# Index scores of a sparse-attention layer: rectified in place in four PSUM banks, in groups of four with one projection tile behind each

## The reference, cut to what matters

```python
h = x @ w_in                                  # q, k, v, z, qi, ki, wi are column ranges of h
rel = relu(einsum('bthd,bsd->bths', qi_b, ki))             # 8 index heads
score = einsum('bths,bth->bts', rel, wi_b) * INDEX_SCALE   # weighted sum over the heads
score = where(causal, score, -inf)
_, idx = top_k(score, 128)
logits = einsum('bthd,btjd->bthj', q_b, k_sel) * ATTN_SCALE
o = softmax(logits) @ v_sel                   # 16 heads of width 128
out = (o * silu(z)) @ w_out
```

## Time and profile before

| | us |
|---|---|
| Time before, median of 3 runs | 1727.27 (1726.52 to 1730.99) |
| The profiled execution, its own time | 1730.23 |
| Its span in the trace | 1728.2 |
| TensorE busy, share of the span | 1597.8 (92%) |
| VectorE busy | 709.0 (41%) |
| ScalarE busy | 526.3 (30%) |
| GpSimd busy | 589.1 (34%) |

### The profile page before, as it was taken

One profiled execution on the slowest core, in us unless ns is written; L12 is line 12 of the kernel. 1 busy time (PEld: TensorE's weight loads), 2 busy tenths in 40 slices (PEclk: granted clock), 3 DMA queues, 4 the chain that ended last, 5 costly groups with the idle time before them and its releaser, 6 DMA issues. The chain is left out here.

```text
span 1728.2 us, 23481 instructions
## 1 busy us (share of the span) xinstructions
PE 1597.8 (92%) x9937; PEld 1342.5 (78%) x9937; DVE 709.0 (41%) x1399; ACT 526.3 (30%) x850; POOL 589.1 (34%) x244
## 2 busy tenths in 40 slices
PE   6998999999999988999998999899999787968998
PEld 6896885998979854778787997897887643557997
DVE  4031440331163545885544135312401556478524
ACT  3444224332223222244443123433221234331210
POOL 5333320343423274444642423242442350422021
PEclk9998999999999998999999999999999776567999
DMA  4313220224223221220112322442331000020111
GB/s 151 92 55 98 73 72 3 74 94 177 84 74 98 86 85 38 74 93 30 49 49 85 124 74 86 147 105 74 98 98 49 1 1 0 0 69 5 50 50 49
DMA packets 115970, 121.60 MB, mean 70 GB/s; under 512 B 14623, under 2 KB 109833, under 8 KB 115610
## 3 DMA queue, kind: packets, MB, share of 16 engines
q1 hardware_dynamic: 112320, 114.16, 20.9%
q10 hardware_dynamic: 3546, 5.94, 0.9%
HBM read 113.80 MB, written 6.29 MB: 69 GB/s over the span
## 5 line engine op out<-in xcount | busy, mean ns | idle before, releaser
L193 POOL TENSOR_TENSOR w_low<-w_ring,w_high 128x2048 fp32r<-128x2048 f32 (+1 forms) x92 | 419.4, 4559 | 844.7 <-ACT w_high L184 844.7
L209 PE MATMUL ps<-w_high,xT_high 128*128 128x256 f32 (+1 forms) x1056 | 303.6, 287 | 7.8 <-POOL w_low L193 3.4
L209 PE MATMUL ps<-w_high,xT_low 128*128 128x256 f32 (+1 forms) x1056 | 298.4, 283 | 0.0
L209 PE MATMUL ps<-w_low,xT_high 128*128 128x256 f32 (+1 forms) x1056 | 298.3, 282 | 0.0
L184 ACT ACTIVATE w_high<-w_ring 128x2048 fp32r<-128x2048 f32 (+1 forms) x92 | 173.5, 1887 | 369.7 <-PE ps L209 356.6
L209 PE MATMUL ps<-xT_high,w_high 128*128 128x512 f32 (+3 forms) x624 | 253.8, 407 | 8.7 <-DVE mix_a L742 7.7
L209 PE MATMUL ps<-xT_high,w_low 128*128 128x512 f32 (+3 forms) x624 | 249.5, 400 | 0.0
L209 PE MATMUL ps<-xT_low,w_high 128*128 128x512 f32 (+3 forms) x624 | 249.0, 399 | 0.0
L209 PEld LDWEIGHTS ps<-w_high,xT_high 128*128 128x128 f32 x1056 | 202.1, 191 | 15.4 <-POOL w_low L193 8.2
L209 PEld LDWEIGHTS ps<-w_low,xT_high 128*128 128x128 f32 x1056 | 202.0, 191 | 1.8 <-issue 1.7
L209 PEld LDWEIGHTS ps<-w_high,xT_low 128*128 128x128 f32 x1056 | 201.7, 191 | 0.0
(11 more groups left out here) (507 smaller groups left out, 2449.3 us busy)
## 6 DMA issues: line engine op xcount, KB each, us to landing
w_ring<-in_gla_w_in_dram SPq DMA_DIRECT2D x24, 1024.0 KB, 5.3
w_ring<-in_dsa_w_in_dram SPq DMA_DIRECT2D x19, 1024.0 KB, 5.1
w_ring<-in_w_in_dram SPq DMA_DIRECT2D x18, 1024.0 KB, 5.2
w_ring<-in_gla_w_out_dram SPq DMA_DIRECT2D x8, 1024.0 KB, 5.0
w_ring<-in_ple_gate_w_dram SPq DMA_DIRECT2D x8, 1024.0 KB, 5.1
w_ring<-in_dsa_w_out_dram SPq DMA_DIRECT2D x8, 1024.0 KB, 5.2
x_scratch<-x SPq DMA_DIRECT2D x4, 1024.0 KB, 6.8
w_ring<-in_w_out_dram SPq DMA_DIRECT2D x4, 768.0 KB, 4.7
```

Of the source, the lines that this page charges most:

```text
L193: self.nc.gpsimd.tensor_tensor(self.slot(self.w_low, i % RING, k, cols), self.slot(self.w_ring, n % RING, k, cols), self.slot(self.w_high, ...
L209: return self.nc.tensor.matmul(out, lhs, rhs, start=first, stop=last, skip_group_check=not check)
```

## The change

Four score banks instead of two, and no `relu` tile: ScalarE rectifies each score bank in place, and VectorE reads the sums' operand from PSUM. TensorE's wait for the rectified m-2 becomes one for the summed m-4, and ScalarE's wait for a free slot is gone. A projection now follows every fourth product, so six projections (4 to 9) stand among the scores where four (4 to 7) stood, with their copies, shuffles and rotations, and `n_scores` becomes 10.

```diff
-        relu = probT[:, 0:2]
+        score_bank = lambda m: m % 4
...
-        n_scores = DSA_HEADS // 2
+        n_group = 4
+        n_scores = n_group + 3 * IDX_HEADS // n_group
...
-                    if m >= 2:
-                        pe.wait_ge(sem["relu"], past["relu"] + m - 1)
+                    if m >= 4:
+                        pe.wait_ge(sem["summed"], past["summed"] + m - 3)
...
-                    g.product(ps[:, m % 2, 0:n], qiT[rows, h // 2, j * P:(j + 1) * P], kiT[rows, 0:n]).then_inc(sem["index_ready"], add("index_ready", 1))
-                    if m % 6 == 5 and 4 + m // 6 < n_scores:
-                        project(4 + m // 6)
+                    g.product(ps[:, score_bank(m), 0:n], qiT[rows, h // 2, j * P:(j + 1) * P], kiT[rows, 0:n]).then_inc(sem["index_ready"], add("index_ready", 1))
+                    if m % n_group == n_group - 1:
+                        project(4 + m // n_group)
...
-                    if m >= 2:
-                        act.wait_ge(sem["summed"], past["summed"] + m - 1)
-                    nc.scalar.activation(relu[:, m % 2, 0:n], ps[:, m % 2, 0:n], ACT.Relu).then_inc(sem["relu"], add("relu", 1))
+                    nc.scalar.activation(ps[:, score_bank(m), 0:n], ps[:, score_bank(m), 0:n], ACT.Relu).then_inc(sem["relu"], add("relu", 1))
...
-                    r, w, s = relu[:, m % 2, 0:n], wi[:, j, h:h + 1], score[:, j, 0:n]
+                    r, w, s = ps[:, score_bank(m), 0:n], wi[:, j, h:h + 1], score[:, j, 0:n]
```

More of the change, by code:

```diff
@@ L1345, in logits @@
                         pe.wait_ge(sem["kT_rotated"], past["kT_rotated"] + 1)
-                        pe.wait_ge(sem["relu"], past["relu"] + len(pairs))
+                        pe.wait_ge(sem["summed"], past["summed"] + len(pairs))
                     for j in range(NT):
@@ L1533, in _ @@
                     ins.then_inc(sem["summed"], add("summed", 1))
-                    if m % 6 == 5 and 4 + m // 6 < n_scores:
-                        swap_query(4 + m // 6)
+                    if m % n_group == n_group - 1:
+                        swap_query(4 + m // n_group)
                 dve.wait_ge(sem["summed"], past["summed"] + len(pairs))
```

## The result

| | us |
|---|---|
| The changed kernel, median of 4 runs | 1710.45 (1709.39 to 1712.26) |
| The kernel before, median of 4 runs | 1728.99 (1726.52 to 1730.99) |
| Ratio | 0.9894 (95% interval 0.9876 to 0.9913) |
| The profiled execution: its time, its span | 1709.88, 1708.0 |

The change takes 1.1% off, 18.3 us of 1728.99 by the ratio. The spans differ by 20.2 us, but the first score product, which the change can't move, begins at 636.75 us before and at 633.10 after. Those 3.65 us come from other times at the low clock well before the scores: the mean clock of the first 170 us is 0.93 before and 0.95 after, 2.6 of the 3.65 us are there by 116 us, and they are not the change's. From the first score product on the changed kernel gains 17.1 us, and the offset stays within 0.1 us of that through the head loop.

What follows compares the result with a forecast made beforehand. Bound: a two-slot ring of three engines, VectorE slowest, in the score stretch; TensorE later. Selection 17.9 us earlier less 2.0 at the restart gives 15.9 off the 1727.3 median: 1711.4 us, range 1707 to 1721.

Steps and rivals of the forecast that it cites:

- The stretch on TensorE: Score stretch: six projections and 24 scores take 44.7 us instead of 62.6, ending 17.9 us earlier.
- The term of the scores: Score products on TensorE: each group flows as two pairs, four pairs of each width, 9.8 us in all.
- the changes between scores and projections: TensorE in the score stretch: switching from projection to scores and back costs about 0.2 us a group, 1.2 in all.
- Rectifying in place: ScalarE writing the PSUM bank it reads: priced like the write into SBUF, 0.60 us for 512 columns.
- Rivals A and C: Score stretch: products go one behind the other, 1721 us (12 in 100); ScalarE's in-place write is slow, 1738 (4 in 100).
- The thinnest cover: GpSimd in the score stretch: rotation 7 done at about 676, shuffle 9, which waits for it, due at 682.
- The selection: VectorE after the score stretch: starts 17.9 us earlier, at 683.0, takes 66.0 us as before, ends at 749.0.
- 11 us idle: TensorE before the head loop: after ten projections and two logit tiles it stands until the first mask, 11 us.
- The restart: Selection's end to first turned probability: 5.0 us plus 2.3 for the low clock, against 5.3 before, 2.0 lost.
- Rival B: Head loop's start: the low clock lasts past project 20, costing 5 us, time 1715 us; 10 in 100.
- Behind it: Head loop: TensorE is busy 126 of 126 us, so the 15.9 us shift carries through to the end.
- had the sums kept their present length: VectorE in the score stretch: unshortened sums, 35.8 us and two more shuffles, would still fit into 44.7 us.

Runs made afterwards that it cites:

- six_banks: Changed kernel with six score banks, groups of six and four projections in the score stretch; ratio to the kernel before 0.9819, then 0.9809.
- warm: Changed kernel with 42 unused filler matmuls on TensorE in its idle gap before the logits; ratio to the kernel before 0.9882, restart 5.1 us.
- sbuf4: Changed kernel, but ScalarE rectifies into four SBUF slots and VectorE reads the sums' operand there; ratio to the kernel before 1.0029.
- move_only: Kernel before with only the order changed: groups of four, six projections in the stretch, two banks and two SBUF slots; ratio 0.9998, stretch 61.8 us.
- psum_only: Kernel before with only the rectified scores' place changed: in place in two PSUM banks, groups of six, four projections; ratio 0.998, stretch 63.8 us.
- four_six: Changed kernel with groups of six and four projections in the stretch, four PSUM banks kept; ratio to the kernel before 0.9869, stretch 46.8 us.

## Why the prediction was right

The forecast was 1711.4 us and 15.9 us of gain; the trace shows 17.1, the runs 1710.45. That the two times lie within 1 us is in part luck: 1711.4 counts from a median of 1727.27 before, and beside the changed kernel that median was 1728.99, so that the runs' own gain is 18.3 us. The figure to compare is the trace's. By the prediction's own steps:

- *The stretch on TensorE*: the copy of query 9 begins at 676.93. Less the 0.2 us that the prediction puts between projection and copy, TensorE's part is 43.6 us against the forecast 44.7. The term of the scores was 9.8 and is 2 x (1.07 + 1.49 + 1.92) = 9.0 us; the other 0.3 us are the changes between scores and projections. The stretch got 19.0 us shorter, not 17.9; this 1.1 us is nearly the whole miss.
- *Rectifying in place*: 0.582 us for 512 columns against 0.597 into SBUF. A sum takes 0.750, not 0.69. Both lie beside projections. Rivals A and C didn't come.
- *The thinnest cover*: rotation 7 ends at 672.5 and shuffle 9 begins at 677.57, so 5.1 us were left where the prediction had some 6. GpSimd was busy for 40.3 of 43.9 us.
- *The selection*: 66.0 us, unchanged.
- *11 us idle*: 11.09. That it is the two projections moved ahead is shown by six_banks, which puts them back and loses the gap.
- *The restart*: 7.3 forecast, 7.3 measured, of which 2.1 are the clock (warm). Rival B didn't come: the clock is 0.50 from 745 to 750 and 0.98 from 750 to 755.
- *Behind it*: the head loop takes 165.7 us in both.

One step failed, though the sum didn't rest on it: "had the sums kept their present length, its 35.8 us and two more shuffles would still fit into 44.7, with a `w_low` at worst pushing one group past its end by a us or two". With the sums in SBUF, and the waits of sbuf4, the stretch is 64.0 us, not near 45. The step took VectorE's busy time from a stretch with four projections. Six projections bring more `w_low` and rotations with them: GpSimd is busy for 44.3 us in sbuf4 and 44.4 in move_only, but 30.0 before and 27.7 in psum_only. Each of them holds VectorE, which was then busy 46.2 us and not 35.8 plus 1.5. And the step didn't ask where in a group the holds fall: the multiplication and three sums of sbuf4's third group last 9.2 us, longer than the 7.4 us of a group.

So the PSUM operand carries the change together with the banks: place alone has the ratio 0.998, banks in SBUF 1.0029, both together 0.989. The new order isn't needed for it. Alone it has 0.9998, and four_six, with both but the old order, has 0.9869 and 118.1 us by the stages against 118.4.

## What to carry to other kernels

In a ring of engines, the number of slots and the length of the slowest step act together: two changes that each bring nothing alone were worth 1% together, so try the whole before dropping the parts, and then take parts out of the whole, since a third one may not be needed. Work moved ahead of a serial chain on another engine is missing behind it; count what still covers that chain, and choose the split at which both chains end together (here four projections in front and twelve behind, with six banks, 13.9 us better than the change itself by the stages). And when a held engine is costed, count the holder's work in the new stretch, with all that was moved into it, not in the old one.

## What the runs showed of the hardware that was not expected

A VectorE multiplication with a single SBUF tensor was held for 4.57 us beside a GpSimd operation of 4.62 us; with its input in PSUM it took 0.62. The Trainium skill has a rule for this in "GPSIMD Engine Reference", section "1. Specifications": the two engines share SBUF interfaces, in conflict where VectorE has two SBUF inputs or runs in a mode that uses both ports. The trace agrees for the sums, with two SBUF tensors: up to 4.68 us in sbuf4. The multiplication can only be of the second kind, and no trace names the mode; when not held, it took 0.47 us for 512 columns from SBUF in the kernel before and 0.75 us from PSUM in the changed one, which fits a faster mode. Products in opposite row halves also ran in pairs when four or six stood in a row: twelve records of 512 columns in 2.85 us, where one product alone takes 1.12.
